# Gated feed-forward layers: pairs of inner blocks by seven quarter products in place of eight, with the weights mixed on GpSimd

## The reference, cut to what matters

```python
h = rms_norm(x, ffn_norm_w[layer])
gu = h @ w_gate_up[layer]
x = x + (jax.nn.silu(gu[..., :FFN_DIM]) * gu[..., FFN_DIM:]) @ w_down[layer]
```

## Time and profile before

| | us |
|---|---|
| median of 3 runs (1258.83 to 1259.7) | 1259.23 |
| the profiled execution's own time | 1260.43 |
| its span, first to last instruction | 1259.1 |
| TensorE busy | 1245.2 (99%) |
| VectorE busy | 804.3 (64%) |
| ScalarE busy | 686.0 (54%) |
| GpSimd busy | 124.6 (10%) |
| HBM traffic | 174 GB/s over the span |
| mean granted TensorE clock | 0.998 of full speed |

### The profile page before, as it was taken

How to read it: one execution, slowest core, us unless ns; L and a number is a source line. 1 busy time by engine, 2 the same in 40 slices (tenths; PEclk the granted TensorE clock), 3 DMA queues, 4 the chain that set the end, 5 groups by cost and what they waited for, 6 DMA issues and landing times.

```text
span 1259.1 us, 17913 instructions
## 1 busy us (share of the span) xinstructions
PE 1245.2 (99%) x7322; PEld 1046.3 (83%) x7322; DVE 804.3 (64%) x1086; ACT 686.0 (54%) x1017; POOL 124.6 (10%) x113
## 2 busy tenths in 40 slices
PE   8999999999999999999999999999999999999997
PEld 6888888888888888888888887888888888899896
DVE  5657755566788566565566988846875765654543
ACT  6665544443777644444447766546855363644543
POOL 1130000000221200000000312000320000100001
PEclk9999999999999999999999999999999999999999
DMA  8755476865454658655546444333456544566661
GB/s 280 230 168 180 143 229 200 265 184 174 143 166 153 218 153 252 200 183 178 182 130 208 157 131 140 116 102 102 134 192 243 179 143 131 176 208 186 185 199 52
DMA packets 119218, 220.21 MB, mean 175 GB/s; under 512 B 8304, under 2 KB 54128, under 8 KB 119136
## 3 DMA queue, kind: packets, MB, share of 16 engines
q1 hardware_dynamic: 115312, 206.08, 51.5%
q0 software_dynamic: 2672, 10.20, 2.5%
q10 hardware_dynamic: 1152, 2.78, 0.6%
HBM read 215.88 MB, written 3.15 MB: 174 GB/s over the span
## 4 chain that ended last, share of the span: by engine, by line
PE 96%; DMA 1%; ACT 1%; DVE 1%; issue 0%; SPq 0%; ACTq 0%; DVEq 0%
PE ps L395 25%; PE ps L397 25%; PE ps L396 25%; PE ps L477 2%; PE ps L478 2%; PE ps L476 2%; PE ps L793 1%; PE ps L412 1%; PE ps L651 1%; PE ps L781 1%; PE ps L1048 1%; PE ps L770 1%; PE ps L1033 1%; PE ps L753 0%; DMA raw<-in_w_gate_up 0%; PE ps L424 0%
## 5 line engine op out<-in xcount | busy, mean ns | idle before, releaser
L1565 DVE TENSOR_TENSOR spl<-raw,spl 128x1024 fp32r<-128x1024 f32 x387 | 475.7, 1251 | 163.7 <-ACT spl L1081 162.4
L1081 ACT CAST spl<-raw 128x1024 fp32r<-128x1024 f32 x387 | 399.8, 1050 | 206.4 <-PE ps L397 94.9
L395 PE MATMUL ps<-spl,xs 128*128 128x512 f32 x928 | 371.3, 400 | 0.0
L397 PE MATMUL ps<-spl,xs 128*128 128x512 f32 x928 | 362.1, 390 | 0.0
L396 PE MATMUL ps<-spl,xs 128*128 128x512 f32 x928 | 361.4, 389 | 0.0
L397 PEld LDWEIGHTS ps<-spl,xs 128*128 128x128 f32 x928 | 174.2, 188 | 37.3
L395 PEld LDWEIGHTS ps<-spl,xs 128*128 128x128 f32 x928 | 174.4, 188 | 35.7 <-issue 1.5
L396 PEld LDWEIGHTS ps<-spl,xs 128*128 128x128 f32 x928 | 174.6, 188 | 34.2 <-issue 0.5
L395 PE MATMUL ps<-spl,ys 128*128 128x512 f32 x496 | 199.4, 402 | 0.1
L397 PE MATMUL ps<-spl,ys 128*128 128x512 f32 x496 | 194.3, 392 | 0.0
L396 PE MATMUL ps<-spl,ys 128*128 128x512 f32 x496 | 194.1, 391 | 0.0
(11 more groups left out here) (324 smaller groups left out, 1210.2 us busy)
## 6 DMA issues: line engine op xcount, KB each, us to landing
raw<-in_w_in SPq DMA_DIRECT2D x112, 512.0 KB, 3.8
raw<-in_w_gate_up SPq DMA_DIRECT2D x176, 256.0 KB, 4.2
raw<-in_mlp_w SPq DMA_DIRECT2D x64, 512.0 KB, 4.3
raw<-in_w_down SPq DMA_DIRECT2D x44, 512.0 KB, 4.4
raw<-in_w_out SPq DMA_DIRECT2D x24, 512.0 KB, 4.2
raw<-in_xattn_wk SPq DMA_DIRECT2D x8, 512.0 KB, 4.0
raw<-in_xattn_wv SPq DMA_DIRECT2D x8, 512.0 KB, 4.4
raw<-in_w_branch_gdn SPq DMA_DIRECT2D x8, 512.0 KB, 3.3
```

What stands on the lines that cost most here:

```text
L395: self.do.matmul(bank, xh, hi, start=start, stop=False)
L397: m = self.do.matmul(bank, xl, hi, start=False, stop=stop)
L1081: self.do.copy(self.k.spl[:, u % NH, 0, :], self.k.raw[:, u % NR, :]).then_inc(*self.up("hi", (u,)))
L1565: self.do.tensor_tensor(lo, self.k.raw[:, u % NR, :], hi.bitcast(F32), ALU.subtract).then_inc(*self.up("lo", (u,)))
```

## The change

Blocks 0, 1 and 2 stay as they are. Blocks 3 to 10 are taken in four pairs (`p` = 1 to 4). A pair is a product of 256 tokens x 1024 by 1024 x 1024 weights; tokens, inner dimension and columns are each halved, and the eight quarter products are replaced by seven (Winograd's form of Strassen's algorithm). The sums of activations that it wants (`S1` to `S4`) are made once for a layer by GpSimd (`mix`), transposed (`mix_turn`) and split. The sums of weights (T5, T7, T6, T4) are made for each pair by GpSimd in place, in scratch slots into which the weights are now loaded (`bring_pair`, `pair_mix`): two halves of 128 x 1024 for each. Each product (`pair_product`) takes two units of weights, which ScalarE and VectorE split as before, and has 2 x 6 matmuls of 128 x 512. The results are added up in SBUF tiles `pa` and `pb`: three by ScalarE copies (`pair_copy`), four by VectorE adds from PSUM (`pair_sum`), and three sums of 128 x 512 by GpSimd (`pair_rest`). `pair_gated` is `gated` with the tiles in SBUF in place of PSUM. In a pair the order is 1, 2, 5, 3, 7, 6, 4, with three or four units of `w_down` between. The loads of the pieces and of the `w_down` units stand in one list on SyncE; `ask` puts loads of the ring ahead of pieces.

In the cut below `mix`, `pair_mix` (128 x 1024) and `pair_rest` (128 x 512) are GpSimd's, `pair_product` is TensorE's, `pair_sum` (one input in PSUM, one in SBUF), `pair_gated` (both inputs in SBUF) and `ahead` are VectorE's; the last piece is from `ffn`.

```diff
+    def mix(self, n):
...
+        self.do.tensor_tensor(s[1], h[1][:, top], h[1][:, low], ALU.add).then_inc(*self.up("pm", ("S", n, 1)))
+        self.wait_ge(*self.at("pm", "S", n, 1))
+        self.do.tensor_tensor(s[2], s[1], h[0][:, top], ALU.subtract).then_inc(*self.up("pm", ("S", n, 2)))
...
+    def pair_mix(self, l, p, i, h, *split):
+        b11, b12, b21, b22 = (self.s(f"{name}{h}_{l}{p}") for name in PIECES)
+        x, y, o = {5: (b12, b11, b11), 7: (b22, b12, b12), 6: (b22, b11, b11), 4: (b21, b11, b21)}[i]
+        for name in {5: (0, 1), 7: (3,), 6: (), 4: ()}[i]:
+            self.wait_ge(*self.at(f"ld_wb{2 * name + h}", l, p))
+        if i != 5:
+            self.wait_ge(*self.at("pm", ("T", l, p, {7: 5, 6: 5, 4: 6}[i]), h))
+        for u in split:
+            self.wait_ge(*self.at("lo", u))
+        self.do.tensor_tensor(o, x, y, ALU.subtract).then_inc(*self.up("pm", (("T", l, p, i), h)))
+
+    def pair_rest(self, l, p, n):
+        for event in ((("am", "M", l, p, 1), ("am", "M", l, p, 2)), (("am", "M", l, p, 5), ("dm", "M", l, p, 7)),
+                      (("pm", "sum", l, p, 1),))[n]:
+            self.wait_ge(*self.at(*event))
+        x, y, o, op = ((1, 0, 1, ALU.add), (2, 0, 0, ALU.add), (2, 3, 2, ALU.add))[n]
+        self.do.tensor_tensor(v[o], v[x], v[y], op).then_inc(*self.up("pm", ("sum", l, p, n)))
...
+    def pair_product(self, l, p, i, h):
...
+        self.wait_ge(*self.at("lo", u))
+        o = self.ps(*key)
+        for j in range(2):
+            k = 2 * h + j
+            self.do.matmul(o, x[:, 0, k, :], v[:, 0, j], start=k == 0, stop=False)
+            self.do.matmul(o, x[:, 0, k, :], v[:, 1, j], start=False, stop=False)
+            m = self.do.matmul(o, x[:, 1, k, :], v[:, 0, j], start=False, stop=k == 3)
...
+    def pair_sum(self, l, p, i):
...
+        self.do.tensor_tensor(v[o], self.ps("M", l, p, i), v[x], ALU.add).then_inc(*self.up("dm", ("M", l, p, i)))
+
+    def pair_gated(self, l, b, t):
...
+        self.do.scalar_tensor_tensor(v, v, 1.0, w[:, 0:256], ALU.add, ALU.mult).then_inc(*self.up("dm", ("g0", l, b, t)))
...
+        self.do.scalar_tensor_tensor(o, v, self.small(f"hs{l}{t}", 1), w[:, 256:512], ALU.mult,
...
     def ahead(self, n=LA):
...
-            self.do.tensor_tensor(lo, self.k.raw[:, u % NR, :], hi.bitcast(F32),
+            self.do.tensor_tensor(lo, self.source(u)[0], hi.bitcast(F32),
...
+    for p in range(1, 5):
+        left, right = 2 * p + 1, 2 * p + 2
+        at = {}
+        for i in (1, 2, 5, 3, 7, 6, 4):
+            us = []
+            for h in range(2):
+                us.append(E.u)
+                E.pair_product(l, p, i, h)
...
+                if h and i in (1, 2, 5):
+                    E.pair_copy(l, p, i)
...
+                E.ahead()
+            at[i] = us
+            if i == 1:
+                for h in range(2):
+                    E.pair_mix(l, p, 5, h, us[h])
+                for h in range(2):
+                    E.pair_mix(l, p, 7, h)
+            if i == 2:
+                E.pair_rest(l, p, 0)
...
+                    turn(left - 2)
+                    turn(right - 2)
...
+            if i == 5:
+                for h in range(2):
+                    E.pair_mix(l, p, 6, h, us[h])
+                for h in range(2):
+                    E.pair_mix(l, p, 4, h, at[2][h])
...
+            if i == 7:
+                E.take(f"act{left}")
+                E.pair_gated(l, left, 0)
...
+            if i == 6:
+                E.pair_sum(l, p, 6)
+                E.pair_sum(l, p, 7)
+                E.pair_rest(l, p, 1)
+                E.pair_rest(l, p, 2)
...
+            if i == 4:
+                E.take(f"act{right}")
+                E.pair_sum(l, p, 4)
+                E.pair_gated(l, left, 1)
...
+            if i in ({2: (7, 6, 4), 4: (1, 7, 4)}.get(p, (1, 7, 6, 4))):
+                down(todo.pop(0))
+            if i == 4:
+                finish(p)
```

More of the change, by code:

```diff
@@ L125, in begin @@
         self.dry = dry
-        self.units = []
+        self.units, self.ring, self.loads = [], [], []
         for c in self.count.values():
@@ L238, in s, with source @@
         return self.k.yf[:, i - NSLOT, :]
+    def source(self, u):
+        kind, i, *event = self.k.units[u]
+        if kind == "ring":
+            return self.k.raw[:, i % NR, :], self.at(f"raw{i % NR}", u)
+        return self.k.ar[:, i, :], self.at(*event)
     def s2(self, name):
@@ L320, in after @@
             return
+        if n[:3] == "ffn":
+            self.take(f"sd0_{n}", f"sd1_{n}")
         self.norm_scale(n)
-        for t in range(2):
-            self.give(f"h{t}_{n}", ("sq", n, t))
+        if n[:3] == "ffn":
+            self.take(f"sa_{n}", f"sb_{n}")
+            self.mix(n)
+            for t in range(2):
+                self.give(f"h{t}_{n}", ("pm", "S", n, 4))
+                self.give(f"sd{t}_{n}", ("sq", n, t))
+        else:
+            for t in range(2):
+                self.give(f"h{t}_{n}", ("sq", n, t))
     def cols(self, blk, src, k0, g, xin, ready, release="ev", pre=None):
@@ new lines, in ask, with mix_turn @@
+    def ask(self, n):
+        for _ in range(n):
+            self.k.loads.append(len(self.k.ring) + self.asked)
+            self.asked += 1
+    def mix_turn(self, n, i):
+        b = self.hold("S", n, i)
+        self.wait_ge(*self.at("pm", "S", n, i))
+        v = self.mixed_raw(n, i)
+        for k in range(4):
+            m = self.do.transpose(b[:, k * P:(k + 1) * P], v[:, k * P:(k + 1) * P], self.ident())
+        m.then_inc(*self.up("tp", ("S", n, i)))
+        self.let(("S", n, i), "xl", "S", n, i)
@@ L2242, in weights @@
     def weights(self):
-        for u in range(NR, len(self.k.units)):
-            self.fetch(u)
+        for load in self.k.loads[NR:]:
+            if type(load) is tuple:
+                self.bring_piece(*load)
+            else:
+                self.fetch(load)
     def finish_out(self, t):
@@ L2258 @@
 mem_keys mem_keys_turn ma_norm ma_turn ma_scores softmax ma_sums eight ma_eight ma_out out_norm
+ask mix mix_turn bring_pair pair_mix pair_copy pair_sum pair_gated pair_rest
 ret_turn ret_scores ret_out ret_scale ret_gates ffn_turn mlp_turn mlp_split mlp_factors
@@ L2503, in ffn, with down, turn, mix_turn @@
     wd = E.k.W["w_down"][l]
-    for b in range(NB):
+    def down(d, b=None):
+        E.rows(("fd", l), wd, range(d, d + 1), 0, 1, "ys", place_of(d), lambda t, kt: ("xl", "ft", l, d // 2),
+               d == 0, False, ("dn", l, d))
+        if b:
+            turn(b)
+        E.ahead()
+    def turn(b):
+        E.ffn_turn(l, b)
+        E.give(f"act{b}", ("mx", "ft", l, b))
+    def mix_turn(i):
+        if i == 4:
+            E.take(f"S4_{n}")
+        E.mix_turn(n, i)
+    def bring(p, *names):
+        for name in names:
+            for h in range(2):
+                E.take(f"{name}{h}_{l}{p}")
+                E.bring_pair(l, p, name, h)
+    def finish(p):
+        E.pair_sum(l, p, 3)
+        E.pair_gated(l, 2 * p + 2, 0)
+        E.pair_gated(l, 2 * p + 2, 1)
+        E.give(f"pa{l}{p}", ("dm", ("gu", l, 2 * p + 2), 0), ("dm", ("gu", l, 2 * p + 1), 1))
+        E.give(f"pb{l}{p}", ("dm", ("gu", l, 2 * p + 2), 1), ("dm", ("gu", l, 2 * p + 1), 1))
+    for b in range(3):
         E.take(f"act{b}")
         k0 = 0
+        if b:
+            E.ask(6)
         for g in ONES if b else FIRST:
@@ L2515, in ffn @@
             E.ahead()
[L2516 to L2526 removed]
+            if b == 1 and k0 == 2:
+                turn(0)
+            if b == 2 and k0 < 4:
+                mix_turn((1, 2, 4)[k0 - 1])
@@ new lines, in ffn @@
+            if b == 1 and k0 == 4:
+                bring(1, "b11")
+            if b == 2 and k0 == 1:
+                bring(1, "b12", "b21")
+                E.ask(1)
+                bring(1, "b22")
+                E.ask(1)
+            if b == 2 and k0 == 2:
+                E.give(f"sa_{n}", ("tp", "S", n, 2))
+        if b == 2 and l == 0:
+            E.take("mem2a", "mem2b")
+            E.load_second()
+            E.load_con()
+        if b == 1:
+            down(0)
+            turn(1)
+            down(1)
@@ L2527, in ffn @@
+    E.give(f"S4_{n}", ("mm", "M", l, 4, 3))
+    down(16, 9)
+    down(17, 10)
     E.take("g_" + after)
@@ L2529, in ffn @@
     E.norm(after, after, "X", "xs", ("fd", l))
[L2530 to L2544 removed]
+    down(18)
+    E.ahead(LAST)
+    ends(E, ("fd", l), wd, range(19, 22), 0, 3, "ys", place_of(19),
+         lambda t, kt: ("xl", "ft", l, 9 if kt == place_of(19) else 10), False, after)
 def diff(E):
```

218 lines of the change are left out of this document (175 added, 43 removed).

## The result

The changed kernel takes **1371.09 us** (median of 5 runs, 1369.51 to 1372.71), the kernel before, beside it on the same chip, 1259.7. The ratio is 1.0884, with a 95% interval of 1.0868 to 1.0900: slower by 111.4 us. The prediction said 1376, between 1330 and 1425.

What follows compares the result with a forecast made beforehand. TensorE bounds the kernel before; in the pairs, turns between VectorE and GpSimd would take over. 47 us a pair gave +58.7 a layer, +117 on 1260.4, so 1376 us beside the median, range 1330 to 1425.

Steps and rivals of the forecast that it cites:

- What bounds it: Feed-forward pairs: TensorE bounds before at 33.6 us; afterwards VectorE and GpSimd SBUF instructions take turns, 44.7 us.
- The pair in the row: One pair laid out in queue order with the turn prices: 47 us from product 6 to product 6.
- 4 x 47: A layer's four pairs: each 47 us, less 2.2 for two downs that stand elsewhere, gives 185.8 us.
- the four small mixes of activations (4 x 1.1): GpSimd before the pairs: hidden in two blocks and costing nothing; without that cover, 4.4 us.
- +58.7 for a layer, +117 for both: Both layers: 185.8 us replaces 128.9, plus 1.8 of transposes, equally in each layer.
- The two take turns, one whole instruction each: VectorE instructions with both inputs in SBUF alternate with GpSimd's: splits at 1.11 us, mixes at 2.25.
- TensorE's saving: Gate and up matmuls: 21.8 us less, 3.6 more for transposes, so -18.2 us for two layers.
- the loads: Weight pieces, issued half a pair or more ahead: cost nothing; without cover, 4.2 us for each late piece.
- Rival 1: Pairs: GpSimd and VectorE run side by side, TensorE stays the bound, 1241 us; chance 7%.
- Rival 2: Pairs: TensorE's clock falls to half rate in gaps, 57.0 us a pair, 1440 us, or 1408 if half the time; 12%.
- Rival 3: Pairs: turns are cheaper than laid out as long queues overlap better, 1262 to 1340, say 1300 us; 7%.
- The marks: Profile signs in pairs: splits about 2.5 us mean, mixes 2.3 to 3.4, PSUM sums 0.69, TensorE busy 0.65, pair 47.

Runs made afterwards that it cites:

- write_only: Changed kernel with every GpSimd weight mix and 128x512 sum in the pairs replaced by equally long fills that read nothing: 1249.69 us, ratio 0.9925.
- before_write: Kernel before plus 14 GpSimd fills of 128x1024 in each of blocks 3 to 10: 1260.02 us, ratio 0.9998.
- before_read6: Kernel before plus six unused GpSimd subtractions of 128x1024 in each of blocks 3 to 10: 1311.39 us, ratio 1.0405.
- tiny_all: Changed kernel with GpSimd's weight mixes and sums cut to 8 columns and its four activation mixes per layer made fills: 1242.52 us, ratio 0.9860.
- the two fillers: Changed kernel plus 16, or 9, useless matmuls ahead of product 2 in each pair: 1375.61 us and 1373.29 us.
- woven_early: Against the changed kernel: two pairs per layer, ordinary blocks between products, mixes and sums on VectorE, activation turns issued one part earlier: 1270.76 us, 1.0079 of the kernel before.

## Why the prediction was right

**What bounds it** held. The turns of whole instructions were read off three meetings in the kernel before, and the two runs with fills, *write_only* in the changed kernel and *before_write* in the old one, show that it is GpSimd's reading that makes them. *before_read6*, worked out beforehand as 20.2 us for a block from the same two prices, measured 20.0.

**The pair in the row** held. Laid out were 47 us, and 44.8 with three downs; measured were 46.0 and 45.8, and 44.6. Over three periods that is 138.8 against 136.4, so 2.4 us less for a layer. The prices of 1.1 and 2.25 are right within what the rows can show.

**Three terms were wrong, and they nearly cancelled:**
1. "4 x 47" for a layer. Four pairs have three periods between them; the fourth is the two ends, where VectorE has splits done in advance at the start and no next pair's mixes beside it at the end. In layer 1 the first matmuls of products' steps start from 567.5 to 734.0, 166.5 us, of which 136.5 are the three periods: the ends take 30, TensorE's own time for a pair and not the 47 of the turns. A part of that is given back behind the pairs (in layer 0 TensorE waits 3.1 and 0.4 us for the last gated block), so by the sum below it is some 10 us less a layer.
2. "the four small mixes of activations (4 x 1.1) have the two blocks before the pairs to be done in and cost nothing". They have time there, but they are issued the moment the norm is done, when VectorE has four splits in a row to do and TensorE waits for them. It costs the 4.4 that the prediction named for the case without cover: 8.91 against 4.63, and 7.0 us for both layers by *tiny_all*.
3. "+58.7 for a layer, +117 for both". The layers are not alike. In layer 0 three loads, among them the one whose wait the section on the change calls bookkeeping, hold GpSimd's first mixes back by 11.5 us, so that three mixes more fall into the time in which the splits need their turns: by the prices 6.8 of the 9.4 us between the layers. Another 1.8 are there in *write_only* too, where nothing takes turns. "The two take turns, one whole instruction each" failed once as well, in the same place: a split stood still through four mixes. It took 11.13 and 11.10 us in the two fillers, so it is no accident of one run, and 1.22 in *write_only*. It puts 6.7 us of wait at one matmul, but a sum of turns does not depend on their order, and in that stretch at most 1.4 us are left for it.

Layer 1: 58.7 - 2.4 + 4.3 - 10 = 50.6 (50.1 measured). Layer 0: the same and the 8.2 of that stretch, 58.8 (59.5 measured). The 10 is what is left when the other terms are taken off; only its sign and order are shown by the 30 us. So the agreement of 1376 with 1371 is better than its working, and in part luck.

**TensorE's saving** of 18.2 us and **the loads** at nothing: *tiny_all* takes 1242.5 us against the 1241 of the sum (17.8 us less than the kernel before beside it), so together they are right within 2 us.

**The rivals.** Rival 1 (side by side) fell with the first profile. Rival 2 (the clock) was right that it falls and wrong that it would decide: the granted clock is 0.92 to 0.93 in layer 0's pairs and 0.85 to 0.89 in layer 1's, and part of the matmuls start 0.43 apart, so TensorE is listed as busy for 0.77 of a pair, where 0.65 were forecast. But with 30.9 us of work in 46, half-speed matmuls fit between the turns: pairs at 0.85 and at 0.93 take the same time, and the fillers raised the mean clock and not the speed. The Trainium skill (TensorE: Matmul & The Clock Gate, HAM oscillation) warned of gaps that bring half rate; the trace agrees on the rate, and the time shows no loss by it in the change. In *woven_early* the stretches at 0.83 have no such cover. Rival 3 (cheaper turns, 1300) fell as well: in the pairs queues of four mixes alternate with the splits as the single meetings did.

**The marks.** Forecast were splits of about 2.5 us on the mean in the pairs, at most near 3.4, mixes between 2.3 and 3.4, sums from PSUM at 0.69. Measured: in the pair from 255 to 301 us 18 splits at 1.9; apart from the 11.04 the longest is 3.40 in the timelines shown; mixes 2.33 to 3.42, mean 3.06; sums 0.683. The busy times of VectorE and GpSimd add up to 74 us in the 46. The mean of the splits was put too high, since they come in bursts while GpSimd waits (five at 1.13 from 278.03).

## What to carry to other kernels

An engine with 10% of busy time is not free capacity: before work is given to GpSimd, add the two-input SBUF instructions of VectorE and the SBUF-reading ones of GpSimd as if they were one engine, in each stage, and compare the sum with the bound; here it is 44.7 us against 33.6. An algorithm that halves the matmuls per unit of weights doubles the preparation that each one needs, so count beside the matmuls saved what the other engines pay: 12 matmuls less in a pair, 2.7 us, cost 6 splits and 8 mixes here. And look for small moved work at the places where the bound engine waits, not only at the places where it has cover. Look also at what stands ahead of moved work in its new queue: three loads that had cost nothing held GpSimd's first mixes back by 11.5 us.
